# Decay projection first and in column strips, gate products and decay tree on POOL, first weight tiles by halves, x's last quarter later

## What is computed

```
mk, mv = rms_norm(mem) @ w_k, rms_norm(mem) @ w_v            # 256 memory tokens
h = rms_norm(x)
c_val, c_gate, q, k, v, r, a_lr = split(h @ w_in)             # a_lr has 16 columns
u = c_val * sigmoid(c_gate);  conv = depthwise_conv31(u)      # 512 channels, then LayerNorm, silu
log_a = log_sigmoid(a_lr @ w_alpha + b_alpha) / 16            # decay of each key feature
o = gated_linear_attention(q, k, v, log_a)
x += [conv, rms_norm(o) * silu(r)] @ w_out
x += cross_attention(rms_norm(x), mk, mv)
x += relu(rms_norm(x) @ w_up)^2 @ w_down                      # then a final rms_norm
```

## Time and profile before

| | us |
|---|---|
| median of 3 runs (1456.04 to 1456.56) | 1456.31 |
| profiled execution | 1456.2 |
| its span | 1454.5 |

### The profile page before, as it was taken

How to read it: one execution, slowest core, us unless ns; L and a number is a source line. 1 busy time by engine, 2 the same in 40 slices (tenths; PEclk the granted TensorE clock), 3 DMA queues, 4 the chain that set the end, 5 groups by cost and what they waited for, 6 DMA issues and landing times.

```text
span 1454.5 us, 22506 instructions
## 1 busy us (share of the span) xinstructions
PE 1437.2 (99%) x9501; PEld 1408.8 (97%) x9501; DVE 602.8 (41%) x688; ACT 458.0 (31%) x619; POOL 376.0 (26%) x296
## 2 busy tenths in 40 slices
PE   7999999999999999999999999999999999999998
PEld 7999999998999999889999999999999999999997
DVE  5669999987533555623322111221112211122124
ACT  7522253447522443312232200222002210023224
POOL 6642231125322211003222222222222222222220
PEclk9999999999999999999999999999999999999999
DMA  8511511002523411771111111111111111111113
GB/s 338 165 52 45 58 46 42 30 30 73 207 94 114 153 42 44 247 267 44 48 47 52 44 47 54 44 43 44 58 43 43 43 44 57 44 43 43 44 43 117
DMA packets 47357, 114.06 MB, mean 78 GB/s; under 512 B 7720, under 2 KB 23352, under 8 KB 45888
## 3 DMA queue, kind: packets, MB, share of 16 engines
q1 hardware_dynamic: 47296, 113.17, 24.3%
HBM read 100.85 MB, written 12.30 MB: 78 GB/s over the span
## 4 chain that ended last, share of the span: by engine, by line
PE 96%; DVE 3%; DMA 0%; ACT 0%; issue 0%; SPq 0%; DVEq 0%; ACTq 0%
PE ps L1214 59%; PE ps L1315 14%; PE ps L1609 5%; PE ps L1332 3%; PE m L1285 2%; PE ps L1643 2%; PE ps L1741 1%; PE ps L1562 1%; PE m L1522 1%; PE ps L1351 1%; DVE ps L1903 1%; PE ps L1622 1%; PE m L1437 1%; PE m L1586 1%; PE ps L1553 1%; PE m L1535 1%
## 5 line engine op out<-in xcount | busy, mean ns | idle before, releaser
L620 POOL TENSOR_TENSOR w_split<-w_raw,w_split 128x512 fp32r<-128x512 f32 x232 | 319.2, 1397 | 1041.6 <-ACT w_split L694 1041.5
L1214 PE MATMUL ps<-a_op,w_split 128*128 128x344 f32 x3168 | 499.4, 319 | 0.0
L1214 PEld LDWEIGHTS ps<-a_op,w_split 128*128 128x128 f32 x3168 | 497.8, 188 | 0.5 <-issue 0.5
L1214 PE MATMUL ps<-b_op,w_split 128*128 128x344 f32 x2304 | 362.6, 319 | 0.0
L1214 PEld LDWEIGHTS ps<-b_op,w_split 128*128 128x128 f32 x2304 | 361.7, 188 | 0.2
L1315 PE MATMUL ps<-a_op,w_split 128*128 128x344 f32 x1440 | 233.2, 321 | 0.0
L1315 PEld LDWEIGHTS ps<-a_op,w_split 128*128 128x128 f32 x1440 | 226.5, 188 | 1.7 <-issue 1.4
L694 ACT ACTIVATE w_split<-w_raw 128x1024 fp32r<-128x1024 f32 x117 | 122.7, 1051 | 255.2 <-PE ps L1214 246.0
L1903 DVE SCALAR_TENSOR_TENSOR ps<-conv_in,par,ps 128x1024 f32<-128x1024 f32 x116 | 149.7, 1291 | 3.6
L2289 DVE SCALAR_TENSOR_TENSOR tmp<-ps,rstd 128x1032 f32<-128x1032 f32 x32 | 39.5, 1233 | 215.1 <-PE ps L1214 203.2
L2299 DVE TENSOR_TENSOR x_res<-x_res,ps 128x1032 f32 x24 | 29.5, 1230 | 230.8 <-PE ps L1214 230.8
(11 more groups left out here) (255 smaller groups left out, 1100.7 us busy)
## 6 DMA issues: line engine op xcount, KB each, us to landing
w_raw<-in_wt SPq DMA_DIRECT2D x117, 512.0 KB, 3.5
cache_b<-in_cache_v SPq DMA_DIRECT2D x8, 1024.0 KB, 12.0
x_in<-in_x SPq DMA_DIRECT2D x4, 1032.0 KB, 9.2
x_spill<-x_res SPq DMA_DIRECT2D x8, 516.0 KB, 2.6
w_more<-in_wt SPq DMA_DIRECT2D x8, 512.0 KB, 7.1
cache_a<-in_cache_k SPq DMA_DIRECT2D x2, 2048.0 KB, 11.2
cache_b<-in_cache_k SPq DMA_DIRECT2D x2, 2048.0 KB, 11.9
x_res<-in_x SPq DMA_DIRECT2D x1, 3096.0 KB, 11.0
```

What stands on the lines that cost most here:

```text
L620: gp.tensor_tensor(split(t, slot)[:, 1, part, :], src, split(t, slot)[:, 0, part, :].bitcast(F32), ALU.subtract).then_inc(w_low_done, 1)
L1214: last = pe.matmul(ps[:, c0 // CB, 0:w], w_split[:, slot, wp, k, :], src[:, k, xp, c0:c0 + w], start=(k == 0 and j == 0), stop=(k == KT - ...
```

## The change

- Startup. The first weight tile is loaded and split by halves, with the memory's first half between; the second tile's high part is made by halves too. PE first runs 11 fp32 products of constants. The sums of x's squares move behind the tenth memory tile, and x's last quarter is loaded behind weight tile 8 instead of 7.
- Decay tile. It moves ahead of the conv tiles. It is computed in raw fp32 from the scaled x, without parts: for each block and each half of the k-steps four products with 32 weight columns each, written to four strips of 32 partitions. `w_alpha` is laid out four times, on the same strips with zeros between, so that the logit products sum the strips. The raw weights stay in their slot until the tile is done (a new wait ahead of the load of tile T_IN + 2).
- The logit products all stand behind block 1 of the first conv tile, and the softplus chain follows on ACT and, as the first step of DVE's list, on DVE.
- POOL makes the gate products (each ahead of a `lo`), the decay tree and the two memsets. `lnz` and the sigmoids get places of their own. DVE keeps `sample_taps` and the taps: 16, 16, 16, 40 before the first unit.

```diff
-ORDER = [("kv", n) for n in range(16)] + [("in", i) for i in range(N_IN)]
+ORDER = [("kv", n) for n in range(16)] + [("in", 8)] + [("in", i) for i in range(8)] + [("in", i) for i in range(9, N_IN)]
-    SLOTS.setdefault((PLACE["in", I_K], _j // 2), []).append(("z", _j))
+    SLOTS.setdefault((T_IN + I_C, 1), []).append(("z", _j))
...
@@ sync
+            sp.dma_start(w_raw[:, 0, 0:KT // 2, :], WT[0][:, 0:KT // 2, :]).then_inc(first_half_loaded, 16)
             sp.dma_start(par[:, :], a["par"]).then_inc(params_loaded, 16)
+                if wait and isinstance(t, int) and t == T_IN + 2:
+                    sp.wait_ge(tile_done, T_IN + 1)
-            load_w(0, 0, False)
-            for i in range(2):
-                sp.dma_start(m_raw[:, 4 * i:4 * i + 4, :], a["mem"][:, 4 * i:4 * i + 4, :]).then_inc(m_part[i], 16)
+            sp.dma_start(m_raw[:, 0:4, :], a["mem"][:, 0:4, :]).then_inc(m_part[0], 16)
+            sp.dma_start(w_raw[:, 0, KT // 2:KT, :], WT[0][:, KT // 2:KT, :]).then_inc(w_loaded[0], 16)
+            sp.dma_start(m_raw[:, 4:8, :], a["mem"][:, 4:8, :]).then_inc(m_part[1], 16)
-                if 5 <= t < 8:
-                    load_x(t - 4)
+                if t in (5, 6, 8):
+                    load_x((5, 6, 8).index(t) + 1)
-                    sp.dma_start(walpha[:, :], a["w_alpha"]).then_inc(w_alpha_loaded, 16)
+                    sp.wait_ge(consts_ready, 1)
+                    for g in range(4):
+                        sp.dma_start(walpha[32 * g:32 * g + RANK, :], a["w_alpha"]).then_inc(w_alpha_loaded, 16)
@@ gpsimd
+            def gate_product(m):
+
+                wait_in_tile(gp, I_C + 2 * m + 1)
+                gp.wait_ge(sample_value_read, m + 1)
+                u_ = conv_in[:, m, CW - 1:]
+                gp.tensor_tensor(u_, u_, gate_in[:, m % 2, NS:T], ALU.mult).then_inc(u_ready, 1)
+                gp.tensor_tensor(conv_smp[:, m, :, CW - 1], conv_smp[:, m, :, CW - 1], gate_in[:, m % 2, 0:NS],
+                                 ALU.mult).then_inc(u_ready, 1)
...
+                if isinstance(t, int) and t == T_IN + I_A:
+                    gp.engine_nop().then_inc(w_high_done, 1)
+                    gp.engine_nop().then_inc(w_low_done, 2)
+                    return
...
             for p in range(T_OUT):
+                for m in range(CT):
+                    if p == T_IN + I_C + 2 * m + 1:
+                        gate_product(m)
                 lo(p + 2, p % 2)
+                if p == T_IN + I_C + 2:
+                    decay_tree()
+                if p == T_IN + I_Q:
+                    wait_full(gp, ("z", 2 * NB - 1))
+                    gp.memset(qz[0], 0.0).then_inc(qz_zeroed, 1)
+                    gp.wait_ge(conv_states_stored, 32)
+                    gp.wait_ge(sample_taps_done, CT)
+                    gp.memset(qz[1][:, :], 0.0).then_inc(qz_zeroed, 1)
@@ scalar
+            act.wait_ge(first_half_loaded, 16)
+            half_high(0, 0)
             act.wait_ge(params_loaded, 16)
...
+            mem_high(0, 1, 2, 3)
+            act.wait_ge(w_loaded[0], 16)
+            half_high(0, 1)
+            act.wait_ge(m_part[1], 16)
+            mem_high(4, 5)
+            act.wait_ge(w_loaded[1], 16)
+            half_high(1, 0)
+            mem_high(6, 7)
+            half_high(1, 1)
...
+                    if (i, b) == (I_C, 1):
+                        act.wait_ge(operand_low, 16)
+                        for j in range(2 * NB):
+                            z_read(j)
                         wait_read(act, ("z", 4))
                         wait_read(act, ("z", 5))
-                        act.wait_ge(u_ready, 2 * CT)
-                        link(act.activation(lnz, la[:, :, :], ACT.Abs))
+                        link(act.activation(lnz[:, :, :], la[:, :, :], ACT.Abs))
+                    if (i, b) == (I_C, 2):
+                        link(act.activation(lnz[:, :, :], lnz[:, :, :], ACT.Exp, scale=-1.0))
+                        act.activation(lnz[:, :, :], lnz[:, :, :], ACT.Ln, bias=1.0).then_inc(softplus_ready, 1)
+                    if (i, b) == (I_C + 1, 0):
                         act.wait_ge(log_a_ready, 1)
                         act.activation(la[:, :, :], la[:, :, :], ACT.Exp, scale=1.0 / TAU).then_inc(a_ready, 1)
@@ tensor
             def first_in_tile():
 
                 pe.wait_ge(ps_free, T_IN)
...
+                pe.wait_ge(w_loaded[0], 16 * (T_IN // 4 + 1))
+                for k0 in (0, 4):
+                    pe.wait_ge(x_normed, k0 + 4)
+                    for b in range(NB):
+                        for g in range(4):
+                            last = pe.matmul(PS[0][32 * g:32 * g + 32, b, 0:CB], raw(T_IN)[:, k0 + g, 0:32],
+                                             x_in[:, k0 + g, b * CB:(b + 1) * CB], start=(k0 == 0), stop=(k0 == 4))
+                        if k0 == 4:
+                            last.then_inc(tile_done if b == LAST_BLOCK else block_done, 1)
...
             pe.wait_ge(consts_ready, 1)
+            for _ in range(11):
+                pe.matmul(M[1][:, 0:P], ones[:, :], ident[:, :], start=True, stop=True)
-                if n_kv == 8:
+                if n_kv == 9:
                     x_sums()
@@ vector
+            dve.wait_ge(softplus_ready, 1)
+            dve.scalar_tensor_tensor(out=la[:, :, :], in0=la[:, :, :], scalar=0.0, in1=lnz[:, :, :],
+                                     op0=ALU.min, op1=ALU.subtract).then_inc(log_a_ready, 1)
             for m in range(CT):
-                u_product(m)
-                taps(16 if m < 3 else 26)
...
+                sample_taps(m)
+                taps(16 if m < 3 else 40)
+            dve.wait_ge(tree_ready, 1)
             wait_in_tile(dve, I_V - 1)
```

More of the change, by code:

```diff
@@ L779, in _ @@
             w_high(7, 1)
+            w_high(8, 0)
             square_x(6)
-            w_high(8, 0)
             square_x(7)
-            for t in range(9, 12):
+            for t in range(9, 13):
                 w_high(t, t % 2)
             norm_x()
-            w_high(12, 0)
             w_high(13, 1)
@@ L809, in evict @@
                 signal = ps_free if b == LAST_BLOCK else block_read
-                if i < 8 and i % 2 == 0:
-                    m = i // 2
+                ic = i - I_C
+                if 0 <= ic < 8 and ic % 2 == 0:
+                    m = ic // 2
                     if b == 0:
```

124 lines of the change are left out of this document (49 added, 75 removed).

## The result

| | before | after |
|---|---|---|
| median (range), us | 1456.45 (1455.85 to 1457.17, 16 runs) | 1459.15 (1458.12 to 1460.46, 16 runs) |
| profiled execution, us | 1456.2 | 1458.15 |
| its span, us | 1454.5 | 1456.4 |

The changed kernel takes 1.0018 of the time before, 95% interval 1.0012 to 1.0025. It is slower by 2.7 us, clear of the spread between executions, but just inside the 0.2% that I called no change. The forecast was 1452.9 and the range ended at 1456.6, so the measured time lies 2.5 us beyond the range, on the other side of the time before.

A forecast was written before the change was run, and what follows sets the result against it. PE is nearly always busy but tied to DVE, so of PE's 8.3 us gain only DVE's 3.3 (start worth 0) counted: 1456.2 - 3.3 = 1452.9 us, range 1450.6 to 1456.6.

The forecast's parts named there:

- What bounds the kernel: Whole kernel: PE busy nearly all the time, but less PE work shortens it only as far as DVE comes earlier.
- Start: Startup up to the last memory evacuation at 59.6 us: worth 0 there, bounds -1.0 (earlier) and +1.5 us.
- the 1.3 us that the first tiles were to gain: First memory tiles: the fourth tile starts at 18.1 instead of 19.4 us, a gain of 1.3, bounds 0 and 1.9.
- The decay tile: Decay tile on PE: 48 fp32 pieces in four overlapping strips take 3.6 us instead of 11.35.
- rival (5): Decay tile: strips don't overlap at 344 columns, tile takes 13.9 us, kernel slower at 1463.2 us; chance 0.06.
- Where DVE starts: DVE's taps behind the first gate product: they start at about 99.5 us, 11 us later than before.
- what it loses: DVE from first tap to copy: 14.3 us of work gone, 120.1 left, copy at 219.6 us, 3.3 earlier.
- POOL's and SP's queues: POOL's gate products (2.6 us each) and tree (5 to 7), SP's new wait (about 1): hidden; three descriptor issues 1.3 us.
- Where PE waits: Second score unit: PE waits 5 us for DVE's selects and from there is tied to DVE.
- Behind it order and amounts are unchanged: Behind the second unit's wait: PE and DVE keep their relation, so the 3.3 us gain stays to the end.
- rival (2): Second score unit: PE's wait drops the clock to half rate, costing 2.5 us, 1455.4 us; chance 0.17.
- rival (3): Start: constants leave the clock low or the first tile waits, x's norm 1.5 us later still, 1454.4 us; chance 0.12.

The follow-up runs named there:

- fill_wait: Changed kernel with 18 and 3 fp32 products of constants on PE ahead of the second score unit's two groups, where it would wait; 1458.22 us.
- wide: Changed kernel with the decay tile's products at all 128 weight columns, accumulated in one place without strips; 1469.73 us.
- best: start_x_old plus ACT's last decay Exp behind the second conv tile's last eviction and each DVE sample step behind four taps; 1449.82 us.
- exp_late: Changed kernel with ACT's last Exp of the decays moved behind the second conv tile's last eviction; 1458.12 us.
- pool_wait: Changed kernel with POOL's low part of the second memory tile waiting for the whole high part again; 1456.72 us.
- x_old: Changed kernel with x's sums back behind the ninth memory tile and x's last quarter loaded behind weight tile 7; 1457.42 us.
- the two fillings: fill_wait, and start_x_old with the same products of constants ahead of the second score unit's groups; 1458.22 and 1454.25 us.
- start_x_old: Changed kernel with first tiles whole, old load order, and x's sums and last quarter placed as before; products of constants stay; 1455.24 us.

## Why the prediction was wrong, point by point

**What bounds the kernel** was right: DVE paces PE from the score units on. fill_wait, wide and best show it from three sides.

**Start, the step that failed first.** I gave it 0 at the stage's start, with +1.5 as its worst; it is +3.2 in the profiled execution, and +4.6 to +5.8 in those of fill_wait, exp_late and wide, with the same start. The failed term is the 1.3 us that the first tiles were to gain: the fourth memory tile started at 20.68 us, 1.6 later than before (19.08), not 1.3 earlier. Three things in it were off. (a) Mem's first half landed at 7.35 us, not 5.7, and by ACT's first step on it at 6.7 or later in every profile of the new order. I had divided the bytes taken from ahead of it by 400 GB/s (which gives 5.9, not 5.7); putting it ahead of half a weight tile didn't land it earlier at all. (b) "With POOL's low parts about a microsecond ahead of PE" was counted as harmless. It was what hurt: POOL's early half collided with DVE's low parts of mem, 2.71 us instead of 0.88, and this is the largest piece, 2.4 us in the median by pool_wait: 0.7 directly, the rest most likely by the clock that fell in the second tile. I knew of such collisions, and had priced them for x's low parts and the sample steps, but not here. (c) The constants were to have the clock up from 7.5 us on, and to keep it there. In the changed kernel the matmuls come 0.21 us apart until about 12 us; in fill_wait and exp_late they were quick from the first product on, and the clock then fell inside the broken tile. The terms behind it were about right: one tile more ahead of x's sums (2.8 us) put the scaling at 46.25 us, 4.5 later than before, and 1.2 of that came back by the decay tile, where I had 1.3. x_old, which undoes it, took off the difference, 1.6 us in the profiles and 1.7 in the medians. Inside it lies a wait that I had not looked for: an evacuation queued behind five scales held PE for 1.38 us.

**The decay tile** was right: 3.68 us for 3.6. At full width it takes 14.15. The sample's strips were the row to go by, and for rival (5) it would have taken more than 0.144 us a piece; it was 0.077. The Trainium skill's 3.07 for four row strips (TensorE: Matmul & The Clock Gate, Measured speedup vs the span model) would have given, as an estimate, 4.5 us (13.9 / 3.07); the measurement here is of column strips and it decides.

**Where DVE starts, and what it loses** were right to 0.2 us each, counted from the decay tile's start: 39.66 for 39.8 and 120.26 for 120.1, with one sample step of four contended, as taken. For the first of the two that is luck: POOL's gate products ended at 98.97 us, 36.0 behind the decay tile's start where I had 37.5, and DVE's first sample step took 3.6 us where I had 2.2, since its last addition (1.58 us for 0.23) was held up as well. The two errors cancel. POOL's and SP's queues showed no wait that counts.

**Where PE waits** was right in place and roughly in size, 4.5 us for 5. The second step that failed is the next one: "Behind it order and amounts are unchanged". It took 14.87 us from copy to third unit, not 12.87. The clock fell to 1.2 GHz in the wait, and came back some 5 us behind it. That was rival (2), with 0.17. Its mechanism is shown by the two fillings. Its price, 2.5 us, was about right for PE alone: from second to third unit it took 12.66 us, 10.35 before (225.47 to 235.82). But 0.7 us of these 2.3 are hidden, since with the clock up PE waits for DVE's second select (11.07 us with the filling). Net it was 1.6 in the changed kernel, and 1.0 in start_x_old. The other 0.4 of the 2.0 is the copy and the selects beside POOL's low part. The argument against it, that no stall this long is shown, should have lowered nothing: the one stall in the trace, the idle start, spoke for it. The Trainium skill (TensorE: Matmul & The Clock Gate, HAM oscillation) said as much, and the trace after agrees with 0.50 between 225 and 229 us; other traces show falls with shorter waits too (0.50 in fill_wait from 15 to 18 us).

**The rivals and the range.** Rival (2) and rival (3), the start, both came true, and I had added up each one alone: 0.17 and 0.12, treated as exclusive. With +2.0 behind the copy and +3.2 at the start the profiled time follows. But a case for both would not have been enough: at my own prices it gives 1452.9 + 2.5 + 1.5 = 1456.9 us. What (3) lacked is size, 1.5 us for 3.2 and more, since the collision of POOL with DVE was not in it. The slower side was given to one mechanism, the strips.

## What to carry to other kernels

When a step on a helper engine is made to start earlier, look at what the other engine on the critical path does in that very stretch: here a low part that POOL started 1.3 us earlier (3.9 us behind ACT's first step on mem, 5.3 in pool_wait) cost 2.4 us. When a change lets TensorE run ahead of its pacing engine, count the wait at the meeting point as a loss beyond itself if it is several microseconds long, because the matmuls behind it may run at 1.2 GHz; at the score units two short waits (0.7 and 0.5 us) left the clock up, but in the first memory tile waits of 0.6, 1.1 and 0.8 us did not. And rivals that can come true together need a case of their own in the range.

## What the runs showed of the hardware that I had not expected

- What POOL slows on DVE is a matter of the instruction. Beside POOL's low part the sample product of 248 columns took 1.49 us instead of 0.42, the addition on 8 columns 1.59 instead of 0.27, a product of 8 columns 1.26, a copy of 16 columns 0.62 instead of 0.17; the sum of 248 columns between the first two took 0.41 as ever, and taps, which add up in PSUM, 1.35 and 1.31 (best, right behind the gate product). One POOL instruction of the low part lasts 1.3 to 1.5 us, which would fit a DVE instruction that waits until POOL's is through; that was not tested.
- The granted clock in the rows did not show the idle start's half rate, nor the slow spacing up to 12 us in the changed kernel (1.00 beside 0.21 us), but it did show every later fall (0.50). Until the clock has risen once, only the spacing of matmuls tells it.
- The clock fell with waits much shorter than 4.5 us: 3.09 and 0.53 us (exp_late, second unit), 2.01 us between constants and first product (x_old, 0.50 from 9 to 12 us), and 0.58, 1.10 and 0.80 us in the first tile (fill_wait). It stayed up with 0.66 and 0.51 us (best) and with 0.59, 0.33 and 0.82 us (pool_wait).
- The landing of the same 512 KB transfer at the very start varied by 0.7 us between executions (6.65 to 7.33 us by ACT's first step on it), more than most edits of the start were meant to bring.
